# Splitting the transposed tiles directly: the root mean square moved from the projections' inputs to their outputs

## The reference, cut to what matters

```
u = (x * rsqrt(mean(x*x) + eps) * norm_mix) @ w_in      # 2048 -> 5632 columns
q, f, i, g (HGRN2, 8 heads of 128), q, k, v (16 + 4 + 4 attention heads of 64) = split(u)
f -> sigmoid(f), sigmoid(-f);   q -> q*sigmoid(q);   g -> g*sigmoid(g)
q, k of the attention -> RMS norm per head;   i and v are used as they are
```

## Time and profile before

| | us |
|---|---|
| median of 3 runs | 1397.48 (1397.08 to 1397.88) |
| profiled execution, its own time | 1397.7 |
| span of its instructions | 1395.7 |
| PE busy | 1378.3 (99%) |
| DVE busy | 759.1 (54%) |
| ACT busy | 537.4 (39%) |
| POOL busy | 118.3 (8%) |
| data moved | 231.32 MB, 166 GB/s |

### The profile page before, as it was taken

The page is one execution under the profiler, slowest core; times in us unless marked ns, Lnnn a source line. Parts: engine busy times, 40 slices in busy tenths (PEclk is TensorE's granted clock), DMA queues, the critical chain, the costliest instruction groups (busy, mean ns, idle before and its releaser), DMA issues.

```text
span 1395.7 us, 23747 instructions
## 1 busy us (share of the span) xinstructions
PE 1378.3 (99%) x10363; PEld 1336.2 (96%) x10363; DVE 759.1 (54%) x941; ACT 537.4 (39%) x638; POOL 118.3 (8%) x150
## 2 busy tenths in 40 slices
PE   6999999999999999999999999999999999999998
PEld 4898999999898999999999999999999999999998
DVE  4434764477744757455555454545455554545454
ACT  7335994422234334333333333333333333333331
POOL 2010431203310062000000000000000000000000
PEclk9999999899999999999999999999999999999999
DMA  8695545453774455656555565656565555656551
GB/s 236 182 311 165 148 134 158 134 139 112 205 242 129 151 151 152 177 155 181 152 175 157 162 171 153 180 152 181 151 179 154 173 160 159 174 153 179 152 181 69
DMA packets 320449, 231.32 MB, mean 166 GB/s; under 512 B 5094, under 2 KB 292079, under 8 KB 319770
## 3 DMA queue, kind: packets, MB, share of 16 engines
q1 hardware_dynamic: 314000, 206.06, 51.4%
q0 software_dynamic: 6112, 23.59, 5.3%
q10 hardware_dynamic: 234, 0.16, 0.1%
HBM read 219.99 MB, written 14.97 MB: 168 GB/s over the span
## 4 chain that ended last, share of the span: by engine, by line
PE 98%; DVE 1%; DMA 1%; ACT 0%; ACTq 0%; issue 0%; DVEq 0%
PE acc L1497 30%; PE acc L1501 29%; PE acc L1498 28%; PE mx L1662 2%; PE mx L1452 1%; PE acc L1511 1%; PE acc L1517 1%; DMA reg_a<-in_hgrn_norm_dram 1%; PE mx L1591 0%; PE mx L1563 0%; PE mx L1523 0%; PE mx L1637 0%; PE mx L1957 0%; PE mx L1744 0%; PE mx L1578 0%; PE acc L1514 0%
## 5 line engine op out<-in xcount | busy, mean ns | idle before, releaser
L1497 PE MATMUL acc<-act_h,wh 128*128 128x288 f32 x2208 | 597.8, 300 | 0.0
L1498 PE MATMUL acc<-act_l,wh 128*128 128x288 f32 x2208 | 594.7, 295 | 0.0
L985 DVE TENSOR_TENSOR wl<-raw,wh 128x2048 fp32r<-128x2048 f32 x192 | 440.2, 2293 | 55.2 <-PE acc L1501 48.9
L628 ACT ACTIVATE wh<-raw 128x2048 fp32r<-128x2048 f32 x192 | 366.8, 1911 | 240.4 <-PE acc L1501 228.0
L1497 PEld LDWEIGHTS acc<-act_h,wh 128*128 128x128 f32 x2208 | 416.6, 189 | 5.4 <-issue 4.3
L1498 PEld LDWEIGHTS acc<-act_l,wh 128*128 128x128 f32 x2208 | 416.1, 188 | 0.0
L1501 PE MATMUL acc<-act_h,wl 128*128 128x288 f32 x2208 | 322.7, 298 | 0.0
L1501 PEld LDWEIGHTS acc<-act_h,wl 128*128 128x128 f32 x2208 | 302.0, 189 | 7.3 <-issue 6.7
L1497 PE MATMUL acc<-mix_h,wh 128*128 128x288 f32 x832 | 228.7, 299 | 0.0
L1498 PE MATMUL acc<-mix_l,wh 128*128 128x288 f32 x832 | 227.9, 295 | 0.0
L1497 PEld LDWEIGHTS acc<-mix_h,wh 128*128 128x128 f32 x832 | 157.1, 189 | 2.4 <-issue 2.3
(11 more groups left out here) (260 smaller groups left out, 750.5 us busy)
## 6 DMA issues: line engine op xcount, KB each, us to landing
raw<-in_w_in_dram SPq DMA_DIRECT2D x44, 1024.0 KB, 6.0
raw<-in_w_gate_dram SPq DMA_DIRECT2D x44, 1024.0 KB, 5.6
raw<-in_w_up_dram SPq DMA_DIRECT2D x44, 1024.0 KB, 5.6
raw<-in_w_down_dram SPq DMA_DIRECT2D x44, 1024.0 KB, 5.1
raw<-in_w_out_dram SPq DMA_DIRECT2D x16, 1024.0 KB, 5.5
reg_x<-in_state_hgrn_dram POOLq DMA_DIRECT2D x16, 256.0 KB, 6.3
out_dram<-reg_x POOLq DMA_DIRECT2D x16, 256.0 KB, 3.5
bias_rows<-bias_line POOLq DMA_DIRECT2D x1, 3072.0 KB, 16.1
```

Source lines behind the costliest of these rows:

```text
L628: nc.scalar.activation(wh[:, s % WH, :], raw[:, s % RAW, :], ACT.Copy).then_inc(high_done, 1)
L985: nc.vector.tensor_tensor(wl[:, s % WL, :], raw[:, s % RAW, :], wh[:, s % WH, :].bitcast(F32), ALU.subtract).then_inc(low_done, 1)
L1497: mm(out, w_h[:, i, cols], a_hi[:, place(i), :], start=(i == 0), stop=False)
L1498: mm(out, w_h[:, i, cols], a_lo[:, place(i), :], start=False, stop=False)
```

## The change

The projection now runs on x times `norm_mix` only, and 1/rms multiplies what comes out of it. ACT and DVE make `act_h` and `act_l` straight from the transposed tile in PSUM, the norm weight being the instruction's scale; there are six PSUM slots, and the copies into `xT` are shared (ACT the even tiles, DVE the odd ones). The prompt blocks are loaded in halves, ahead of which `norm_mix` comes in as its own transfer; POOL's small loads wait until x is there. PE begins with eight products of ones, the transpose of `norm_mix`, and eight more such products; the other parameters are transposed after the tiles. `x_squares` and `root` stand behind `high(1)` on ACT, and `spread_rms` in the middle of unit 1. DVE now multiplies every unit by `rstd1` when it takes it out of PSUM, before `low(s + 2)`; ACT's functions read the result from SBUF; what was left of DVE's `evacuate` is `finish`. For i the transposed copies are scaled per token in `v_copy`, which becomes two instructions.

```diff
@@ sync
-            sp.dma_start(xtok[0:TS, 2, :], x_sample...).then_inc(x_in[2], 16)
-            for j in range(2):
-                sp.dma_start(xtok[:, j, :], x_prompt[0, P * j:P * j + P, :]).then_inc(x_in[j], 16)
+            for half in range(2):
+                cols = slice(1024 * half, 1024 * half + 1024)
+                for j in range(2):
+                    sp.dma_start(xtok[:, j, cols], x_prompt[0, P * j:P * j + P, cols]).then_inc(x_in[j][half], 16)
+                if half == 0:
+                    sp.dma_start(xtok[0:TS, 2, :], x_sample...).then_inc(x_in[2][0], 16)
@@ gpsimd
+            for j in range(NTT):
+                pool.wait_ge(x_in[j][-1], 16)
...
+            nc.gpsimd.memset(ones2, 1.0).then_inc(ones_set, 1)
@@ scalar
             def x_tile(k):
+                if k == 0:
+                    act.wait_ge(gain_done, 1)
                 act.wait_ge(xt_done, k + 1)
-                nc.scalar.activation(xT[:, k, :], mx[:, k % 4, 0:T], ACT.Copy).then_inc(xt_copied, 1)
+                nc.scalar.activation(act_h[:, k, :], x_slot[k % 6], ACT.Copy, scale=gains[:, 0, k:k + 1])\
+                    .then_inc(acth_done, 1)
+                if k % 2 == 0:
+                    nc.scalar.activation(xT[:, k, :], x_slot[k % 6], ACT.Copy).then_inc(xt_copied_a, 1)
...
             def evacuate(s):
-                act.wait_ge(unit_done, s + 1)
                 if s < S_F:
                     if s < 10:
+                        act.wait_ge(qkv_done, s + 1)
...
-                        nc.scalar.activation(tmp[:, s % 2, :], ps, ACT.Square).then_inc(qk_sq, 1)
-                    nc.scalar.activation(dst, ps, ACT.Copy).then_inc(qkv_done, 1)
+                        nc.scalar.activation(tmp[:, s % 2, :], src, ACT.Square).then_inc(qk_sq, 1)
...
-            x_squares()
-            for k in range(4):
-                x_tile(k)
-            root(1, x_ssq)
-            for k in range(4, 8):
+            for k in range(12):
                 x_tile(k)
             high(0, None)
-            for k in range(KD):
-                if k < KD - 8:
-                    x_tile(k + 8)
-                x_high(k)
+            for k in range(12, KD):
+                x_tile(k)
             high(1, None)
+            x_squares()
+            root(1, rs)
             high(2, None)
@@ vector
             def norm1():
...
+                for k in range(KD):
+                    if k % 2 == 0:
+                        dve.wait_ge(xt_copied_a, k // 2 + 1)
+                    dve.wait_ge(acth_done, k + 1)
+                    nc.vector.scalar_tensor_tensor(out=act_l[:, k, :], in0=x_slot[k % 6], scalar=gains[:, 0, k:k + 1],
+                                                   in1=act_h[:, k, :].bitcast(F32), op0=ALU.mult, op1=ALU.subtract)\
+                        .then_inc(actl_done, 1)
+                    if k % 2:
+                        nc.vector.tensor_copy(xT[:, k, :], x_slot[k % 6]).then_inc(xt_copied_v, 1)
+                    if k == 12:
+                        low(0, None)
...
+                low(1, None)
                 dve.wait_ge(ssq_done, NTT)
...
             def evacuate(s):
                 ps = acc[bank_in(s)][:, 0:T]
+                dve.wait_ge(unit_done, s + 1)
+                if S_I <= s < S_G:
+                    nc.vector.tensor_tensor(i_s[:, s - S_I, :], ps[:, TP:T], rstd1[:, TP:T], ALU.mult)\
+                        .then_inc(is_made, 1)
+                    return
...
+                nc.vector.tensor_tensor(dst, ps, rstd1[:, :], ALU.mult).then_inc(qkv_done if s < S_F else z_made, 1)
+
+            def finish(s):
...
                 if 0 <= s - S_SM - 1 < NU:
                     new_states(s - S_SM - 1)
+                    finish(s - 1)
...
                 if not (S_SM <= s < S_SM + NU or s == S_FFN - 1):
                     low(s + WL, units_through(s))
+                    finish(s)
@@ tensor
             def x_transpose(k):
-                if k >= 4:
-                    pe.wait_ge(xt_copied, k - 3)
+                if k >= 6:
+                    pe.wait_ge(actl_done, k - 5)
+                    pe.wait_ge(xt_copied_v if k % 2 else xt_copied_a, (k - 6) // 2 + 1)
...
+            pe.wait_ge(ones_set, 1)
+            for _ in range(8):
+                mm(mx[:, 0, 0:P], ones, ones, start=True, stop=True)
             pe.wait_ge(small_in, 16)
-            pe.wait_ge(params_in, 16 * 6)
-            nc.tensor.transpose(acc[3][:, 0:N_ROWS], param_rows, ident[0:N_ROWS, 0:N_ROWS]).then_inc(params_t, 1)
-            for j in range(NTT):
-                pe.wait_ge(x_in[j], 16)
-            pe.wait_ge(ones_set, 1)
+            pe.wait_ge(gain_in, 16)
+            nc.tensor.transpose(acc[3][:, 0:KD], param_rows[0:KD], ident[0:KD, 0:KD]).then_inc(gain_t, 1)
+            for _ in range(8):
+                mm(mx[:, 0, 0:P], ones, ones, start=True, stop=True)
             for k in range(KD):
                 x_transpose(k)
-                if k == 7:
-                    spread_rms()
+            pe.wait_ge(gain_done, 1)
+            pe.wait_ge(params_in, 16 * 5)
+            nc.tensor.transpose(acc[3][:, 0:N_ROWS], param_rows, ident[0:N_ROWS, 0:N_ROWS]).then_inc(params_t, 1)
...
             def in_the_middle(s):
+                if s == 1:
+                    spread_rms()
...
                 elif p < S_Q:
-                    pe.wait_ge(f_sig, p - S_F + 1)
+                    pe.wait_ge(z_made, p - S_F + 1)
```

More of the change, by code:

```diff
@@ L165, in layer_kernel @@
         st = sb("st", [P, 2, 5, 4])
-        ones = sb("ones", [P, P])
+        rstd1 = sb("rstd1", [P, T])
+        rs = sb("rs", [P, NTT])[:, :]
         ident = small[:, 0:128]
@@ L224, in layer_kernel @@
         param_rows = reg_a[0:N_ROWS, 1408:1408 + P]
+        ones = reg_a[:, 1536:1664]
+        ones2 = reg_a[:, 2048:2176]
         v_a = reg_v[:, 0:2048].rearrange("p (j c) -> p j c", j=2)
@@ L249, in layer_kernel @@
         mx = ctx.enter_context(nc.psum_tensor("mx", [P, 4, 512], F32))
+        x_slot = [mx[:, i, 0:T] for i in range(4)] + [acc[1][:, 0:T], acc[2][:, 0:T]]
         sp_bank = [mx[:, 2, 0:256], mx[:, 3, 0:256], acc[2][:, 0:256], acc[3][:, 0:256]]
-        x_in = [sem(f"x_in{j}") for j in range(NTT)]
+        x_in = [[sem(f"x_in{j}_{half}") for half in range(2 if j < 2 else 1)] for j in range(NTT)]
         params_in = sem("params_in")
@@ L474, in _ @@
         def _(pool):
-            nc.gpsimd.memset(ones[:], 1.0).then_inc(ones_set, 1)
+            nc.gpsimd.memset(ones, 1.0).then_inc(ones_set, 1)
+            for j in range(NTT):
+                pool.wait_ge(x_in[j][-1], 16)
             pool.dma_start(bucket_of, c_bucket).then_inc(early_in, 16)
@@ L790, in v_copy @@
                 act.wait_ge(v_t, h + 1)
-                nc.scalar.activation(v_a[:, 0:2, P * h:P * h + P],
-                                     sp_bank[0].rearrange("p (j c) -> p j c", j=2), ACT.Copy)\
-                    .then_inc(v_tokd, 1)
+                for j in range(2):
+                    ins = nc.scalar.activation(v_a[:, j, P * h:P * h + P], sp_bank[0][:, P * j:P * j + P], ACT.Copy,
+                                               scale=rs[:, j:j + 1])
+                ins.then_inc(v_tokd, 1)
             def sampled_keys_copy(g):
@@ L1008, in norm1 @@
                 dve.wait_ge(rms_copied, 1)
-                dve.wait_ge(params_done, 1)
-                for k in range(KD):
-                    dve.wait_ge(xt_copied, k + 1)
-                    nc.vector.scalar_tensor_tensor(out=xn(k), in0=xT[:, k, :], scalar=gains[:, 0, k:k + 1],
-                                                   in1=tmp[:, 6, :], op0=ALU.mult, op1=ALU.mult).then_inc(xn_done, 1)
-                low(0, None)
-                for k in range(KD):
-                    dve.wait_ge(acth_done, k + 1)
-                    nc.vector.tensor_tensor(act_l[:, k, :], xn(k), act_h[:, k, :].bitcast(F32), ALU.subtract)\
-                        .then_inc(actl_done, 1)
@@ L1317, in _ @@
             norm1()
-            low(1, None)
             for s in range(S_FFN):
@@ L1801, in x2_ssq @@
                 pe.wait_ge(sq2_done, 2 * KD - 1)
-                mm(mx[:, 0, 0:T], ones[:, :], tmp[:, 0, :], start=True, stop=True).then_inc(ssq2_done, 1)
+                pe.wait_ge(ones_set, 2)
+                mm(mx[:, 0, 0:T], ones2, tmp[:, 0, :], start=True, stop=True).then_inc(ssq2_done, 1)
             def at_start(s):
@@ L1880, in unit_free @@
                 elif p < S_O:
[L1881 removed]
+                    pe.wait_ge(z_made, 2 * AH + p - S_G + 1)
                 elif p < U_FFN:
```

105 lines of the change are left out of this document (57 added, 48 removed).

## The result

The changed kernel takes 1392.74 us (median of 6 runs, 1390.25 to 1394.24) against 1397.41 (6 runs, 1396.11 to 1397.88): 0.9967 of the time before, 95% interval 0.9956 to 0.9977. It is faster, by 4.7 us instead of the 11.2 forecast, and lies above the predicted range of 1384.5 to 1391.6. The profiled execution took 1394.24 us with a span of 1392.0, 3.7 us less than the span before. In a later series the same kernel came to 1391.36 (7 runs); with both, its executions spread over 3.99 us, and sixteen of the kernel before, in one series, over 2.33.

What follows compares the result with a forecast made beforehand. PE's own work was taken as the bound (98% of the span), its start slow or late. 11.7 us gained at the start less 0.5 in slab 37 gave 11.2: 1386.3 us against the median, range 1384.5 to 1391.6.

Steps and rivals of the forecast that it cites:

- T0: Start of the unbroken run of x's transposes on PE; forecast at 9.0 us, bounds 8.0 to 11.7.
- the prediction's own sign: At the start: the prediction is wrong if the first transpose is at 11 us or later.
- the second eight for 3.8 us at that pace or, by the high level's half, 2.1: PE's second eight products of ones before x's transposes, following `small` and one transpose: 3.8 us or 2.1.
- late and slow: Rival: loads or ones hold PE until 11.6 us and the clock is low; 1393.2 us, chance 0.06.
- From T0 to unit 0: x's transposes at mixed clock levels, ending at 18.5 us; PE starts unit 0 at 18.8.
- Unit 0: First unit on PE: 8.6 us, its last part dense at 2.13 instead of 5.34, ending at 27.4 instead of 38.56.
- Unit 1: Second unit on PE: 48 matmuls and the six of the spread, 7.2 us, ending at 34.6 for 46.3.
- The root's chain: ACT's squares and root, then DVE's products, done at 31.1 us; PE at unit 1's middle at 31.7, covered by 0.6.
- No thin stretch behind unit 0: The clock dip at 38.2 us, 1.3 us, goes with the thin stretch that caused it.
- Slabs 2 to 43: Same PE list; DVE gains 0.46 us per unit, covered, so the additions cost nothing; weights move forward with PE.
- Slab 37: PE waits for DVE's chain there; `finish(36)` put into it adds 0.46 us, at most 0.5.
- the rule I weighed: Skill's clock rule: activity releases the throttle, so transposes behind products of ones should run at the high level throughout.

Runs made afterwards that it cites:

- e4: The changed kernel with the constants ahead of norm_mix on ACT's queue and x_sample ahead of the prompt halves on SP's; 1388.18 us.
- e10: The changed kernel with only one small activation added ahead of the tiles, so that ACT's table is loaded early; 1391.04 us.
- e3: The changed kernel with six of the ten broadcasts of slab 12 put among the matmuls of the same slab; 1393.37 us.
- e1: The changed kernel without the second block of eight products of ones; 1390.88 us.
- e2: The changed kernel with all sixteen products of ones ahead of the wait for the constants and norm_mix; 1391.12 us.
- e6: e4 with all sixteen products of ones ahead of the waits; 1386.42 us.
- e8: e6 with one small activation ahead of the tiles, so that ACT's table is loaded early; 1384.4 us.
- e9: e8 with finish(s - 1) behind sampled_take in the recurrence's slabs; 1383.84 us.
- e11: e4 with one product of ones behind each tile from the sixth on, without the early table load; 1386.9 us.
- e7: e4 with slab 12's six late broadcasts and slab 28's 36 small products among wl matmuls, and finish behind sampled_take from slab 33; 1393.27 us.

## Why the prediction was wrong, by its own steps

*T0, forecast 9.0 with bounds 8.0 to 11.7, measured 13.28: 4.3 of the 6.1 us missing at unit 1.* This is the step that failed, and by the prediction's own sign (a first transpose at 11 or later) it was wrong. I let `small` land at 5.2 because its row of before says 4.0 us, and wrote "with another transfer ahead of it perhaps 7.6". It took 8.5. The row was of a transfer issued first, at 0.74; in the change it is issued second, at 1.20, with the first loads of x already issued. The row for a small transfer behind others stood in the earlier trace rows, 7.03 us, and I used it only for the rival "late and slow". The step "the second eight for 3.8 us at that pace or, by the high level's half, 2.1" had the length right (3.3), but in my sum it hid in the wait for x; with `small` last there was nothing left to hide it. e4 sets the order right and gets 9.07.

*From T0 to unit 0, forecast 9.8, measured 11.25.* I costed the ACT table load only at the root. In the kernel before it was covered; the first ACT work of the change is a tile on the path, so it was exposed. Its own 1.28 us and the clock together are the difference: e10, with the load early, needs 9.45. The sum itself was 0.3 us short: six tiles at 0.33, four at 0.66 and six at 0.865 end at 18.8 and not 18.5. A price was wrong without harm: at the higher level an x transpose is 0.18 us apart from the next, not the 0.109 of the earlier trace rows, three for a tile are 0.54, and ACT needs 0.54 as well (I had 0.58); DVE needs 0.61 (I had 0.66). Why the transposes of the earlier trace rows, of the same size, go faster is open.

*Unit 0, forecast 8.6, measured about 9.0* (4.14 + 2.77 + 2.13): right, with the lower level lasting a little longer. *Unit 1, forecast 7.2, measured 7.1:* right. The root's chain ended with DVE's three small products at 36.15 and PE reached the middle at 37.9: covered by 1.8 us, where I had 0.6. *No thin stretch behind unit 0:* right.

*Slabs 2 to 43, "they cost nothing":* right for DVE's multiplication, the exchange of ACT's and DVE's work and the weights. The list of PE's waits has none for a weight transfer, and the distance from unit to unit is 7.18 us as before. What I missed is the clock: 2.75 us lost in slab 12. I had treated a fall as something that only the start can have, although show one behind a thin stretch, and slab 28 has one in the kernel before too. There the changed kernel got 1.2 us back, because its fall is shorter. Windows of the kernel before, then of the changed one:

```profile
262.00:269.00 7.00, 7.00 (x58) 6.35 (x58) 0.00 (x0) 1.14 (x5) 0.00 (x0) 0.60 0.26 62
269.00:274.00 5.00, 5.00 (x26) 5.00 (x25) 2.42 (x2) 2.42 (x4) 4.58 (x5) 0.54 0.07 11
```

```profile
262.00:269.00 7.00, 7.00 (x39) 6.79 (x39) 1.14 (x3) 1.92 (x7) 3.23 (x3) 0.51 0.00 0
269.00:274.00 5.00, 5.00 (x54) 4.68 (x54) 5.00 (x7) 1.76 (x1) 5.00 (x8) 1.00 0.77 212
```

From slab 27 to 29 it is 29.2 us in the kernel before, in e3 and in e10, and 27.6 to 27.7 in the changed kernel, both times, and in e1, e2, e4 to e6, e8, e9 and e11. That is 1.5 us less, and 0.3 had been lost between slabs 13 and 27. Nothing in the prediction foresaw this gain of 1.2; it is luck.

*Slab 37, forecast 0.46 to 0.5, measured 0.36:* mechanism and place right, as e9 shows.

The sum: 11.7 - 4.3 - 1.45 - 0.35 (both units) = 5.6 at unit 1; - 2.75 in slab 12, + 1.2 in slab 28, - 0.36 in slab 37, 3.7 at the end. Of the rivals, "late as well as slow" (1393.2) came nearest to the 1392.74, though its start was 1.7 us too early and its clock too low for the first tiles. I gave it 0.06, and the range left it out. The direction did not hold by the start: 13.28 is 1.6 us behind the 11.65 of the kernel before. It held by what stands behind the start. From there to unit 0 it is 11.3 us instead of 15.1, unit 0 takes 9.0 instead of 11.8, and unit 1 takes 7.1 instead of 7.8; less the 1.6 that is the 5.6 at unit 1. The prediction had these terms, with another mix of levels in the first.

On the rule I weighed: in e10 the recorded clock is 0.50 in the products of ones and rises to 1.00 at 14.0, behind them, and some 45 transposes then keep 1.00 for 8 us, 0.18 us apart. In e1, which has no second ones, the clock is at 0.50 too when the transposes begin, and they stay there for all of their 13.8 us. So transposes did not release the clock in this kernel, and in some profiles they kept it once it was up. The Trainium skill (TensorE: Matmul & The Clock Gate, "What's actually happening") says that activity releases the throttle; these runs agree with it for the products of ones and not for transposes alone. I had written that it makes no exception for transposes. That holds for this section only: "Part 4: PE-mode transpose" of the same page says that the full clock does not engage for the transpose mode. e1 agrees with that, and the 8 us at 1.00 in e10 do not; whether the transposes here are of that mode is in no row.

## What to carry to other kernels

A landing time read from a trace belongs to its place in the issue order: when a change moves a small transfer that everything waits for, price it by the latest small transfer of the trace (7.03 us here, against the 4.0 that I took and the 8.5 measured), and issue it first. When a change makes an engine's first work part of the critical path, look for that engine's one-time costs (here the table load) and start them in an idle moment (1.8 us off the stretch in e10). After a gain at the start, follow it from stage to stage: here a fall of the clock in slab 12 took up to 2.8 us of it back.

## What the runs showed of the hardware

- Issued second on its queue and 0.46 us later, a transfer of 132 KB took 8.5 us to land instead of 3.9; one of 256 KB, issued behind the first halves of x instead of ahead of them, 8.2 instead of 3.7. Both were moved in one edit (e4).
- An x transpose took 0.287 us at a granted clock of 0.50 (e1) and 0.18 at 1.00 (e10), 1.6 times and not twice.
- A small activation before the first tile moved the 1.28 us table load from 13.9 to 4.6 us and took 1.8 us off the transposes' stretch. The second load, for the root, came at 33.72 and was covered.
- The clock in slab 12 fell in nine of the profiles and stayed in e1, e3, e6 and e7, with PE's list of slab 12 unchanged in e1 and e6. One fall costs 1.4 to 2.8 us. Why e1 and e6 were spared is open, and so is why the kernel before was: no run here settles it.
- Spreading 36 small products among dense ones (e7) went with a clock of 0.50 for 17 us and cost 7 us against e4, where they stand in one block and the clock is at 0.50 for some 6 us.
